# Half pieces of three gate groups between the steps of attention, the inverses and the state recurrence

## What is computed

```python
def token_mixer(h, w_in, fox_fb, pool_w, pool_scale, gdn_conv, gdn_a_log, gdn_dt_bias, gdn_norm, w_branch, w_out):
    proj = h @ w_in
    fox_qkv, fox_f, pool_in, gdn_qkv, gdn_b, gdn_a, gdn_z, gates = jnp.split(proj, offsets, axis=-1)
    branch_a = forgetting_attention(fq, fk, fv, fox_f + fox_fb)        # 8 heads x 64
    branch_b = multiscale_pool(pool_in, pool_w, pool_scale)
    branch_c = gated_deltanet(gdn_qkv, gdn_b, gdn_a, gdn_z, ...)       # 4 heads x 128, chunks of 64
    to_model = jnp.einsum('bsnw,nwd->bsnd', branches, w_branch)
    gate = jax.nn.sigmoid(gates.reshape(B, S, N_BRANCHES, D_MODEL))
    return jnp.sum(gate * to_model, axis=2) @ w_out

# inside gated_deltanet, for each chunk: T = inverse(I + L), u = T @ v_beta, w = T @ (k_beta * exp(g)), and then in order
def step(state, xs):
    v_new = u_c - w_c @ state
    o = (q_c * jnp.exp(g_c)[..., None]) @ state + a_c @ v_new
    state = state * jnp.exp(gl)[..., None, None] + jnp.einsum('bhcd,bhce->bhde', k_dec, v_new)
    return state, o
```

## Time and profile before

| what | value |
|---|---|
| median of 3 runs | 1946.81 us (1946.05 to 1950.1) |
| the profiled execution's own time | 1946.16 us |
| its span | 1944.4 us |
| instructions | 26703 |
| mean granted clock of TensorE | 0.99 |
| TensorE busy | 1743.2 us, 90% |
| VectorE busy | 1385.4 us, 71% |
| ScalarE busy | 915.4 us, 47% |

### The profile page before, as it was taken

One profiled execution on the slowest core, in us unless ns is written; L12 is line 12 of the kernel. 1 busy time (PEld: TensorE's weight loads), 2 busy tenths in 40 slices (PEclk: granted clock), 3 DMA queues, 4 the chain that ended last, 5 costly groups with the idle time before them and its releaser, 6 DMA issues.

```text
span 1944.4 us, 26703 instructions
## 1 busy us (share of the span) xinstructions
PE 1743.2 (90%) x7280; PEld 1018.2 (52%) x7280; DVE 1385.4 (71%) x3865; ACT 915.4 (47%) x2233; POOL 683.1 (35%) x583
## 2 busy tenths in 40 slices
PE   8999999999999878878799999999999998877776
PEld 7987887544444223223289778875454442322222
DVE  5775577977777777776468745679777787777764
ACT  5555452444445444444455555424444454544443
POOL 0100002454443465655301100024444444566553
PEclk9999999999999999999999999999999999999999
DMA  6533479999999999999945335899999999999997
GB/s 241 169 115 89 150 273 367 414 426 427 426 427 396 423 427 427 428 427 427 406 146 171 99 98 153 295 367 408 427 426 427 427 402 424 420 428 427 427 427 305
DMA packets 106731, 660.63 MB, mean 340 GB/s; under 512 B 11888, under 2 KB 12288, under 8 KB 40064
## 3 DMA queue, kind: packets, MB, share of 16 engines
q0 software_dynamic: 75376, 546.57, 67.3%
q1 hardware_dynamic: 31248, 112.74, 17.4%
HBM read 658.20 MB, written 1.06 MB: 339 GB/s over the span
## 4 chain that ended last, share of the span: by engine, by line
PE 31%; issue 24%; DMA 23%; DVE 13%; ACT 7%; POOL 1%; DVEq 1%; ACTq 0%; POOLq 0%; SPq 0%
PE acc L746 11%; DMA arena<-experts_dram,idxu 10%; DMA cst<-experts_dram,stage 8%; DMA arena<-experts_dram,stage 4%; PE acc L765 3%; DVE arena L1527 3%; PE psum L697 2%; DVE arena L1583 2%; PE psum L729 2%; PE psum L666 2%; PE psum L667 2%; PE psum L668 2%; DVE arena L1373 1%; ACT w_hi_r L1084 1%; PE acc L666 1%
## 5 line engine op out<-in xcount | busy, mean ns | idle before, releaser
L765 PE MATMUL acc<-arena 128*128 128x512 f32 x896 | 439.5, 619 | 119.6 <-ACT arena L1187 119.2
L746 PE MATMUL acc<-arena 128*128 128x512 f32 x896 | 412.2, 601 | 27.9 <-ACT arena L1161 27.8
L632 POOL DMA_INDIRECT arena<-experts_dram,stage x224 | 312.3, 1394 | 218.3 <-PE acc L765 167.5
L1557 DVE CUSTOM_DVE_ANT_0 arena<-arena,h 128x1024 f32<-128x1024 f32 x224 | 274.6, 1226 | 137.0 <-issue 59.7
L765 PEld LDWEIGHTS acc<-arena 128*128 128x128 f32 x896 | 157.3, 193 | 400.1 <-issue 399.9
L614 POOL DMA_INDIRECT arena<-experts_dram,idxu x224 | 247.5, 1105 | 304.5 <-PE acc L746 276.0
L1527 DVE CUSTOM_DVE_ANT_0 arena<-arena,h 128x1024 f32<-128x1024 f32 x224 | 274.7, 1226 | 105.8 <-DMA arena<-experts_dram,idxu 102.0
L746 PEld LDWEIGHTS acc<-arena 128*128 128x128 f32 x896 | 163.2, 190 | 255.7 <-issue 152.0
L1434 DVE TENSOR_TENSOR raw_r<-raw,w_hi_r 128x1024 fp32r<-128x1024 f32 x152 | 180.2, 1221 | 81.6 <-ACT w_hi_r L1084 80.8
L1181 ACT ACTIVATE gel<-dots 128x1 f32<-128x1 f32 x256 | 51.7, 202 | 296.0 <-DVE dots L1557 295.5
L1084 ACT ACTIVATE w_hi_r<-raw 128x1024 fp32r<-128x1024 f32 x152 | 154.1, 1052 | 61.6 <-DMA raw<-weights_dram 56.6
(11 more groups left out here) (295 smaller groups left out, 2763.1 us busy)
## 6 DMA issues: line engine op xcount, KB each, us to landing
raw<-weights_dram SPq DMA_DIRECT2D x168, 512.0 KB, 3.6
arena<-weights_dram SPq DMA_DIRECT2D x20, 512.0 KB, 6.5
w_hi<-weights_dram SPq DMA_DIRECT2D x12, 512.0 KB, 6.6
lnr<-lnrows_dram POOLq DMA_DIRECT2D x4, 1024.0 KB, 6.5
arena<-experts_dram,idxu POOLq DMA_INDIRECT x224, 13.2
arena<-experts_dram,stage POOLq DMA_INDIRECT x224, 13.5
lnr<-cum_dram POOLq DMA_DIRECT2D x2, 1024.0 KB, 9.1
cst<-weights_dram SPq DMA_DIRECT2D x4, 512.0 KB, 5.5
```

The source lines that it names most:

```text
L632: nc.gpsimd.indirect_dma_start(slots[i % RING][:, :], None, experts[:, :], bass.IndirectOffsetOnAxis(stage[:, i:i + 1], 0)).then_inc(slot_ ...
L746: last = mm(acc[:, c * 512:(c + 1) * 512], diag[:, i % 4, :], slots[n % RING][:, D + c * 512:D + (c + 1) * 512], start=n == 0, stop=n == R ...
L765: last = mm(acc[:, c * 512:(c + 1) * 512], diag[:, i % 4, :], slots[i % RING][:, D + c * 512:D + (c + 1) * 512], start=False, stop=ends)
L1557: nc.vector.tensor_tensor_reduce(slots[i % RING][:, 0:D], slots[i % RING][:, 0:D], h[:, b, :], 1.0, 0.0, ALU.mult, ALU.add, dots[:, i:i + ...
```

## The change

The groups `wide` become three: the other half of branch A's gate joins as `wide` 2. Each step is now a half piece, `("wide", i, j, b)`, of six matmuls for one token block, and `wide_out` is one copy for one block; that of `wide` 2 applies the sigmoid while it copies. Semaphore counts follow. `late` is as it was. The order is written out anew: `attend(k)` issues `fo` of pair k-3, `pt` of pair k-2 and `fs` of pair k, so that a pair takes three turns, and `gated(n)` gives the next n half pieces. After the recurrence's last step, the two other gates and the branches' maps follow one after another. The arithmetic, the weights and the number of matmuls are the same.

```diff
     def br(n):
         return [[("br", n, c, b) for b in range(2)] for c in range(2)]
 
-    chain = []
+    halves = [("wide", i, j, b) for i in range(3) for j in range(4) for b in range(2)][2:]
+
+    def gated(n):
+
+        out = []
+        for step in [halves.pop(0) for _ in range(n)]:
+            out += [step] + ([("wide_out", step[1], step[3])] if step[2] == 3 and step[1] < 2 else [])
+        return out
+
+    def attend(k):
+
+        out = [("fo", *divmod(k - 3, 4))] if k >= 3 else []
+        out += [("foT", (k - 6) // 4)] if k in (6, 10) else []
+        out += [("pt", *divmod(k - 2, 4))] if 2 <= k < 10 else []
+        return out + (fs(*divmod(k, 4)) if k < 8 else [])
+
     for lev in range(1, LEVELS):
-        chain.append([("y", lev, c) for c in range(2)])
-        chain.append([(k, lev, c) for k in (("ty", "uy") if lev < LEVELS - 1 else ("uy",)) for c in range(2)])
...
-    fill += [[("foT", 0), ("wide", 1, 3), ("wide_out", 1)], [("fo", 1, 0), ("pt", 1, 1)] + fs(1, 2), [("fo", 1, 1), ("pt", 1, 2)] + fs(1, 3) + [("late",)]]
-    fill += [gate(0)[1], [("pt", 1, 3), ("fo", 1, 2)], [("fo", 1, 3)], [("foT", 1)]]
-    fill += gate(1) + br(0) + [[]] + br(1) + [gate(2)[0], [("oT", 0), ("oT", 1)], gate(2)[1]]
...
+        s += [("y", lev, c) for c in range(2)] + attend(lev - 1) + gated(1)
+        s += [(k, lev, c) for k in (("ty", "uy") if lev < LEVELS - 1 else ("uy",)) for c in range(2)] + gated(2)
+    s += [("wT", 0), ("wT", 1)] + attend(5) + gated(1)
+    s += [("vn", 0, 0)] + attend(6) + gated(1) + [("o", 0, 0), ("dS", 0, 0)] + gated(1)
+    s += [("vn", 0, 1)] + attend(7) + [("late",), ("o", 0, 1), ("dS", 0, 1)] + gated(1)
+    s += [("vn", 1, 0), ("onorm", 0)] + attend(8) + gated(1) + [("o", 1, 0), ("dS", 1, 0)] + gated(1)
+    s += [("vn", 1, 1)] + attend(9) + [("o", 1, 1), ("onorm", 1)] + gated(1) + [("wide_out", 2, 0), ("wide_out", 2, 1)] + attend(10)
+    for group in gate(1) + br(0) + br(1) + [gate(2)[0], [("oT", 0), ("oT", 1)], gate(2)[1]]:
+        s += group
...
-            def gate_piece(L, g, j, blocks):
+            def gate_piece(L, g, j, ps, b):
 
                 w = split(L, g, j)
-                for ps, b in blocks:
-                    for i in range(2):
-                        k = 2 * j + i
...
-                read(L, g, j, ends[1])
+                for i in range(2):
+                    k = 2 * j + i
...
+                if b:
+                    read(L, g, j, ends[b])
...
                     if kind == "wide":
-                        _, i, j = step
+                        _, i, j, b = step
                         if j == 0 and i:
-                            pe.wait_ge(wide_drained, NB * (2 * L + i))
...
+                            pe.wait_ge(wide_drained, NB * (3 * L + i - 1) + b + 1)
...
                     if kind == "wide_out":
...
+                        _, i, b = step
+                        act.wait_ge(wide_filled, NB * (3 * L + i) + b + 1)
+                        to = (zs[:, b, :], first_gate[:, b, :], gates[:, 0, b, 512:D])[i]
+                        AC(to, acc[:, b * 512:(b + 1) * 512], ACT.Sigmoid if i == 2 else ACT.Copy).then_inc(wide_drained, 1)
...
-                        dve.wait_ge(*(drained(L, ("gate", n, c, b)) if n + c else (late_ready, 2 * L + 2)))
+                        if n:
+                            dve.wait_ge(*drained(L, ("gate", n, c, b)))
+                        else:
+                            dve.wait_ge(*((wide_drained, NB * (3 * L + 2) + b + 1) if c else (late_ready, 2 * L + 2)))
```

40 lines of the change are left out of this document (12 added, 28 removed).

## The result

The changed kernel takes 1975.6 us (median of 6 runs, 1971.35 to 1982.12), the kernel before in the same rounds 1948.24 us (median of 6, 1946.05 to 1950.1). The ratio is 1.0141, with a 95% interval of 1.0128 to 1.0153: slower, as forecast, but by 1.4% and not by 1.0%, and 0.6 us above the upper end of the range. The profiled execution took 1971.35 us (span 1969.5, before 1944.4), and is the shortest of the six.

The account below looks back on a forecast made before the run. TensorE, busy for 90% of the span, bounds the kernel. Per layer 11.7 (waits) + 0.9 (in and out) + 3.4 (clock) - 4.8 - 1.7 (removed) = +9.5 us, two layers +19.0: 1966 us, range 1955 to 1975.

Parts of the forecast that it names:

- The bound and what is removed: First `wide` to `gate(1)`: TensorE 90% busy; 4.8 us of waits and 1.7 of low clock go per layer.
- The waits added: Five places per layer from `y` of level 1 to `foT` (1) where TensorE newly waits: 11.7 us per layer.
- level 5: Inverses: `wT` waits behind a split and additions on VectorE, 0.8 us, taken as 0.9 with a wait at `wide` 2.
- Going in and out: From `t0` to `oT`, 19 runs of dense matmuls instead of 14, 0.2 us each: +0.9 us per layer.
- The clock: Behind the new waits TensorE's clock falls twice per layer, 1.7 us each: +3.4 us.
- The slower side of the forecast, three or four falls: Waits as forecast, three or four clock falls per layer: 1969 to 1973 us; chance within the forecast's shared 0.76.
- Banks largely hidden: Waits at `dS` (0,0) and `vn` (1,0) cost half, one clock fall less: 1955.2 us; chance 0.10.
- Faster (1940): ScalarE frees `vn`'s banks in time, only the waits at `y` and level 5 stay: -3.3 us per layer; chance 0.07.
- places 3 to 5: Waits at `foT` (0) with `dS` (0,0) 2.6, `vn` (1,0) 4.6, `foT` (1) 2.2 us: 9.4 per layer.
- Splits too late: Splits queue behind `late` and `onorm` on ScalarE, so pieces come late: 2.75 us per layer, 1971.5 us; chance 0.02.
- A drain behind each table load: `late` and the wait of `vn` (1,0) grow by 2.8 us per layer: 1971.6 us; chance 0.01.
- The stretch to `gate(1)`: From the first `wide` piece, 80.3 us grow by some 7 of recurrence turns, 0.8 going in and out, and 9.5.

Follow-up runs that it names:

- experiment 5: Changed kernel with two more in-place copies of 1024 elements at the head of `late`, values unchanged: 1982.16 us, ratio 1.017.
- experiments 1 to 3: Three edits of the changed kernel; the first put `late` behind `o` (0,1) and `dS` (0,1): 1970.41 us, ratio 1.0112. The others: experiment 2, experiment 3.
- experiment 4: Changed kernel with a half piece between `t0` and `y` of level 1, taken from ahead of `o` (1,0): 1974.96 us, ratio 1.0139.
- experiment 7: Changed kernel with `fo` (0,3) ahead of `vn` (0,0), `late` behind `gate(1)`'s first half, both `onorm` behind its second: 1942.86 us, ratio 0.9963.
- Experiments 7 and 9: experiment 7, and that kernel with `wT`'s half piece moved between `t0` and `y`, `fo` (1,3) ahead of the last half piece: 1936.96 us, ratio 0.9941.
- the second trace (11): The changed kernel run once more with no edit, for a second trace: 1976.22 us, ratio 1.014.
- experiment 6: Changed kernel with the last three half pieces directly behind `vn` (1,0), instead of one in each of three gaps: 1987.74 us, ratio 1.0187.
- experiment 3: Changed kernel with `fo` (0,3) ahead of `vn` (0,0) instead of behind it: 1965.6 us, ratio 1.0091.
- experiment 2: Changed kernel with `late` and both `onorm` moved behind the last `foT`, after the whole recurrence: 1957.43 us, ratio 1.0051.

## Why the prediction was right and wrong

**The bound and what is removed.** Right. The 4.8 us of waits of the earlier trace rows went in both layers. The low clock of the earlier trace rows went with them in layer 1; in layer 2 the clock fell close by, behind the new wait of `dS` (0,0).

**The waits added.** Right at all five places, forecast against measured: `y` 1.4 and 1.4; `wT` and level 5 0.9 and 0.5; `foT` (0) with `dS` (0,0) 2.6 and 2.6; `vn` (1,0) 4.6 and 4.6; `foT` (1) 2.2 and 2.3. The sum is 11.7 against 11.4. At level 5 the path of ScalarE and VectorE came out as counted (`wT` starts 164.15 - 155.01 = 9.1 us behind `y`), and TensorE arrived 0.3 us later than counted. Counting the path of ScalarE from `fs` to the copy that frees the bank, and that of TensorE to the same point, was enough; experiment 5 lengthened the first by what two copies take and the wait followed, and experiments 1 to 3 removed single waits as this count says. In experiment 4 the count missed the split ahead of `foT` (0).

**Going in and out.** 0.9 us per layer were forecast. With the clock up, experiment 7 leaves 138.4 for the new order; before leaves 143.2 - 4.8 - 0.47 x 3.4 = 136.8. That is 1.6 us. Experiments 7 and 9, both of the new order, lie 0.5 us apart here, so the remaining 0.7 is about as small as the method resolves.

**The clock: the step that failed.** The prediction said "The longest is well above the stretch that did it, and 2.1 and 2.2 are nearest to it, though in one piece; I take two falls, +3.4 us", at 1.7 us each. The number of falls was nearly right (two in layer 1, three in layer 2). Their size was not: 1.7 us was read behind the earlier trace rows, where 48 dense matmuls follow at once and the clock was back after 3.4 us. The change has taken just this group away. Behind `vn` (1,0) now stand small matmuls and half pieces of six, and the clock stayed low for 10.2 us each time. The term measured 0.47 x (13.7 - 2.6) = 5.2 us in layer 1 and 0.47 x (20.5 - 0.7) = 9.3 in layer 2, 7.2 on the mean, not 3.4; in the second trace (11) it is 9.2 and 9.0. With 7.2 the forecast would have been 1966 + 7.6 = 1973.6.

What sets the length of a fall is shown in part. In all these traces together eleven falls have long dense work beside or directly behind them (the 48 matmuls of before, or `gate(1)`), and each lasted 3.4 us. The 31 falls between the turns lasted 3.4 to 17.1 us. But the 18 dense matmuls of experiment 6 shortened nothing, and behind the wait of 4.6 us at `vn` (1,0) the clock was low for 6.8, 10.2, 13.7 or 17.1 us in the kernels that have it, in experiment 3 for 17.1 and 6.8 in the two layers of one execution. That more than dense work decides is certain; what it is stays open.

**The sum again, with what was measured,** both layers: waits 2 x (11.4 - 4.8) = 13.2; clock 5.2 + 9.3 - 2 x 1.6 = 11.3; that leaves 3.3 of the 27.85 observed for the going in and out, for which 2 x 1.6 was read above (from the same stretches, so this is no second proof). Forecast were 19.0: 13.8, 3.4 and 1.8.

**The rivals.** The slower side of the forecast, three or four falls (1969 to 1973), came nearest, and still priced a fall at 1.7 us. Banks largely hidden (1955): false, 2.1 and 4.6 us stand in full. Faster (1940): its point, that places 3 to 5 and the clock stay under 3.3 us, was missed by far, 9.5 + 7.2 us; experiment 7 meets it (1.2 us for `foT` and `vn` (0,1), the clock at 1.00) and is faster, at 1942.86. Splits too late: not in the changed kernel, but in experiment 2. A drain behind each table load: false. SiLU starts 188.59 - (187.29 + 1.28) = 0.02 us behind the end of its load, and `vn` (1,0) waited 4.58 us, not 7.4. "ScalarE: Activation LUTs" of the Trainium skill, section "What ACT_TABLE_LOAD costs", adds a drain of about 1.38 us to each load; this trace does not agree.

**The stretch to `gate(1)`,** forecast to grow from 80.3 by 7, 0.8 and 9.5 to 97.6 us, is 214.95 - 116.10 = 98.9 in layer 1 and 1196.61 - 1094.25 = 102.4 in layer 2. (One reading of the prediction is wrong and changes nothing: dense pieces stand back to back behind `foT` (1) in the changed kernel only, 240 matmuls up to `oT`; before, `vn`, `o` and `dS` lie between their groups.)

**What stays open.** Why the clock falls behind one wait of 2.05 us and not behind the same wait 978 us earlier or in another execution, and how long it then stays low. Experiments 3, 6 (two layers, 6.8 and 3.4 us behind the same wait of `dS`) and 11 show it again. All waits were the same there to 0.1 us, so no view of waits tells it, and the forecast of such an execution can't be better than some 3 us per layer.

## What to carry to other kernels

Before you cut a dense group into cover for small steps, look at what the group covered besides: here 48 matmuls hid ScalarE's `late` (4.7 us), and the clock was back 3.4 us after its fall; with one half piece of 1.5 us neither was so. Do not carry the price of a fall of the clock over from the row in which it was seen in the old order: behind it stood dense work, and where the new order has small matmuls there it lasted up to five times as long. What kept the clock up here was an order with no wait above 1.4 us (experiments 7 and 9). Then treat each wait on a bank as two paths to one point, and move the long block of the other engine (`late`, `onorm`) behind work that is dense: with one `fo` this turned a kernel 1.4% slower into one 0.4% faster, and a half piece moved from `wT` to `t0` (with one more `fo`) made it 0.6%.

## What the runs showed of the hardware that was not expected

- **A low clock lasts, and its price is partial.** Stretches at 1.2 GHz lasted 3.4 us where long dense work stood beside or directly behind them (11 of 11), and 3.4 to 17.1 us between small matmuls and half pieces (31). What of it lay inside a wait cost nothing. Each other us cost 0.45 to 0.49 in the changed kernel and experiments 1 and 3 to 6, a little under the half that a halved clock takes from work that goes by it; part of the small matmuls' time does not: `pt` (L1008) takes 0.71 us to the next start at 1.2 GHz (199.10 - 198.39), 0.54 at 2.4 (183.75 - 183.21).
- **A fall needed no long wait.** It fell behind 2.05, 2.6 and 1.31 us of idleness with small matmuls around them, and never in experiments 7 and 9, whose longest waits are 1.4 and 1.0 us. Once it fell inside a wait of 2.4 us between dense matmuls (experiment 2, layer 2). The length alone does not decide: behind the 1.4 us of `y`, at the start of the inverses, the clock fell in no kernel, behind the 1.31 us of `vn` (1,1) in both layers of experiment 6, and behind the 2.05 us of `dS` (0,0) not each time. "TensorE: Matmul & The Clock Gate" of the Trainium skill, section "A second HAM failure mode: psum-queue depth-cycling", tells of a kernel in which short idle times between groups of matmuls, from its turns through PSUM banks, were enough to make the clock go up and down; the traces here agree for idle times of 1.31 to 2.6 us, and experiments 7 and 9 show shorter ones that were not enough.
- **The same program, the same waits, another clock.** 13.7 and 20.5 us in two layers of one execution, 20.5 and 20.5 in another. The runs of the changed kernel spread over 10.8 us (1971.35 to 1982.12), those of `late_in_gates` over 1.6 (1942.47 to 1944.09) and those of `half_taken_at_wT`, whose trace has no low clock in the stretches either, over 4.8 (1934.83 to 1939.6).
